# Reordering the hand-over from expert scores to expert outputs, and two operands of the routing copied to PSUM

## The reference, cut to what matters

```python
v1, i1 = lax.top_k(s1, PEER_TOPK)          # 8 heads, 128 keys each, 16 best
v2, i2 = lax.top_k(s2, PEER_TOPK)
cand = (v1[..., :, None] + v2[..., None, :]).reshape(T, PEER_HEADS, 256)
sc, pos = lax.top_k(cand, PEER_TOPK)
eidx = jnp.take_along_axis(cidx, pos, axis=-1)
gate = jax.nn.softmax(sc, axis=-1)
u = jnp.take(u_tab, eb, axis=0)
a = jnp.einsum('nhkd,nd->nhk', u, xb)
w = jax.nn.gelu(a, approximate=False) * gb
vv = jnp.take(v_tab, eb, axis=0)
return jnp.einsum('nhk,nhkd->nd', w, vv)
```

## Time and profile before

| | us |
|---|---|
| median of 3 runs (1568.36 to 1580.45) | 1569.83 |
| the profiled execution | 1577.24 |
| its span, first to last instruction | 1575.6 |
| PE busy in the span | 1510.4 |
| DVE, POOL, ACT busy | 1025.4, 997.6, 652.0 |

### The profile page before, as it was taken

The page is one execution under the profiler, slowest core; times in us unless marked ns, Lnnn a source line. Parts: engine busy times, 40 slices in busy tenths (PEclk is TensorE's granted clock), DMA queues, the critical chain, the costliest instruction groups (busy, mean ns, idle before and its releaser), DMA issues.

```text
span 1575.6 us, 25142 instructions
## 1 busy us (share of the span) xinstructions
PE 1510.4 (96%) x8005; PEld 1348.5 (86%) x8005; DVE 1025.4 (65%) x2027; ACT 652.0 (41%) x1013; POOL 997.6 (63%) x611
## 2 busy tenths in 40 slices
PE   7998989999999989999999999899999999999995
PEld 4777767888999989999999999878888888888884
DVE  5356576588999987776767673465555555555556
ACT  5555562234333344555555554223333333333332
POOL 3313241234686866767676667688888888888873
PEclk9999999999999999999999999999999999999998
DMA  6112130222686878998999899799999999999991
GB/s 221 55 54 94 46 102 1 100 88 85 193 277 207 271 245 311 332 324 320 345 332 327 310 347 346 236 336 343 352 347 345 352 345 341 356 343 344 354 323 54
DMA packets 155442, 397.92 MB, mean 253 GB/s; under 512 B 12992, under 2 KB 77248, under 8 KB 153216
## 3 DMA queue, kind: packets, MB, share of 16 engines
q1 hardware_dynamic: 117936, 262.93, 49.1%
q0 software_dynamic: 37456, 134.37, 22.5%
HBM read 347.12 MB, written 50.14 MB: 252 GB/s over the span
## 4 chain that ended last, share of the span: by engine, by line
PE 78%; DVE 14%; issue 4%; ACT 3%; POOL 1%; DMA 1%; DVEq 0%; ACTq 0%; SPq 0%; POOLq 0%
PE banks L1504 12%; PE banks L1506 12%; PE banks L1505 12%; PE banks L1450 11%; PE banks L1452 11%; PE banks L1451 11%; PE banks L1711 5%; PE banks L1566 2%; DVE cand L1248 1%; DVE sel L1258 1%; DVE work L1253 1%; ACT hi L365 1%; DVE rows L1135 1%; DVE top_i L1223 1%; DVE top_i L1208 1%
## 5 line engine op out<-in xcount | busy, mean ns | idle before, releaser
L371 POOL TENSOR_TENSOR lo<-raw,hi 128x1024 fp32r<-128x1024 f32 x292 | 704.2, 2413 | 447.7 <-ACT hi L365 437.6
L1450 PE MATMUL banks<-x1T_hi,hi 128*128 128x384 f32 (+2 forms) x1168 | 405.0, 347 | 5.4 <-POOL lo L371 5.1
L1452 PE MATMUL banks<-x1T_hi,lo 128*128 128x384 f32 (+2 forms) x1168 | 399.0, 342 | 0.0
L1451 PE MATMUL banks<-x1T_lo,hi 128*128 128x384 f32 (+2 forms) x1168 | 398.7, 341 | 0.0
L365 ACT ACTIVATE hi<-raw 128x1024 fp32r<-128x1024 f32 x292 | 306.0, 1048 | 1.2 <-PE banks L1506 0.7
L1504 PE MATMUL banks<-hi,wgt_hi 128*128 128x512 f32 x768 | 302.3, 394 | 3.6 <-DVE wgt_lo L1359 3.6
L1506 PE MATMUL banks<-hi,wgt_lo 128*128 128x512 f32 x768 | 303.3, 395 | 0.0
L1505 PE MATMUL banks<-lo,wgt_hi 128*128 128x512 f32 x768 | 302.6, 394 | 0.0
L1450 PEld LDWEIGHTS banks<-x1T_hi,hi 128*128 128x128 f32 x1168 | 221.1, 189 | 10.2 <-issue 5.7
L1359 DVE TENSOR_TENSOR wgt_lo<-wgt,wgt_hi 128x384 fp32r<-128x384 f32 x128 | 72.4, 566 | 240.0 <-ACT wgt_hi L901 184.3
L1452 PEld LDWEIGHTS banks<-x1T_hi,lo 128*128 128x128 f32 x1168 | 220.6, 189 | 4.9
(11 more groups left out here) (184 smaller groups left out, 1825.0 us busy)
## 6 DMA issues: line engine op xcount, KB each, us to landing
raw<-u_t SPq DMA_DIRECT2D x128, 512.0 KB
raw<-v_tab SPq DMA_DIRECT2D x128, 512.0 KB
g_scratch<-stage SPq DMA_DIRECT2D x12, 2048.0 KB
gg<-g_scratch SPq DMA_DIRECT2D x32, 768.0 KB
gelu_scratch<-gelu SPq DMA_DIRECT2D x116, 192.0 KB
ga<-gelu_scratch SPq DMA_DIRECT2D x29, 768.0 KB
raw<-w SPq DMA_DIRECT2D x26, 512.0 KB
raw<-w_pq SPq DMA_DIRECT2D x16, 512.0 KB
```

The costliest lines, as they stand in the source:

```text
L371: eng.tensor_tensor(l[:, :], raw[:, c % RAW_SLOTS, :], h[:, :].bitcast(F32), ALU.subtract).then_inc(lo_ready, 1)
L1450: pe.matmul(o, h[:, s], hiT[:, k, tokens], start=(k == 0), stop=False)
L1451: pe.matmul(o, h[:, s], loT[:, k, tokens], start=False, stop=False)
L1452: ins = pe.matmul(o, l[:, s], hiT[:, k, tokens], start=False, stop=(k == KT - 1))
```

## The change

Three parts. In `route_block` an operand of the sum of candidates and one of the gates' logits are copied to PSUM first (`best_1`, `top_1`), with one more wait on `route_step`; ROUTE_STEPS counts them. On DVE the eight dots of round 15 stand ahead of the waits and the first two products, and read `x1_home`; behind wgt_lo of tiles 0 and 1 the products 2 and 3 are made too, and `octet(0)` makes neither again. On ACT the gelu of the dots moves ahead of wgt_hi of tiles 0 and 1, so ahead of the last four gelus of u. PE's wait before v tile 0 asks for all 128 used rows, where it asked for 120, since banks 4 and 5, in which x1_home lies, are written by v tile 0.

```diff
--- before.py
+++ after.py
@@ -81,7 +81,7 @@
 assert len(FIRST_ROWS_AT) == R_PRE * ROWS + AHEAD
 LIST_SLOTS = 4
 LIST_STEPS = 4
-ROUTE_STEPS = 2 + 5 + 2 + 2 + 6
+ROUTE_STEPS = 3 + 5 + 3 + 2 + 6
 X_CHUNKS = 4
 
 
@@ -221,6 +221,8 @@
         iota_home = banks[:, 6, 0:NKEY]
         best_f = banks[:, 6, NKEY:NKEY + LISTS * TOPK].rearrange("p (l k) -> p l k", l=LISTS)
         pos_f = banks[:, 7, 0:2 * P].rearrange("p (s n) -> p s n", s=2)
+        best_1 = banks[:, 7, 2 * P:3 * P].rearrange("p (h k) -> p h k", k=TOPK)
+        top_1 = banks[:, 7, 3 * P:3 * P + PH].rearrange("p (h k) -> p h k", k=1)
         gateT = banks[:, 6, NKEY:NKEY + DENSE]
 
         y0 = banks[:, 0:2, :].rearrange("p h n -> p (h n)")
@@ -902,13 +904,12 @@
 
             for it in range((A_PRE + A_MID) // 4, ETILES // 4):
                 if it == ETILES // 4 - 1:
+                    act.wait_ge(dots8_free, R_ALL + 1)
+                    act.activation(dots_gelu[:, :], dots[:, :], ACT.Gelu).then_inc(dots_gelu_ready, 1)
                     weight_hi(0, 0, True)
                     weight_hi(1, 0, True)
                 for k in range(4):
                     gelu_tile(k, it, keep=4 * it + k - A_PRE - A_MID)
-
-            act.wait_ge(dots8_free, R_ALL + 1)
-            act.activation(dots_gelu[:, :], dots[:, :], ACT.Gelu).then_inc(dots_gelu_ready, 1)
 
             with act.Fori(0, ETILES // 8 - 1) as i:
                 for k in range(8):
@@ -1130,9 +1131,7 @@
                 if k == 0:
 
                     dve.wait_ge(dots8_free, r + 1)
-
-                with_x = x1[:, 0, :] if isinstance(r, int) and r == R_ALL - 1 else x1_home
-                dve.tensor_tensor_reduce(rows[:, k, :], rows[:, k, :], with_x, 1.0, 0.0, ALU.mult, ALU.add,
+                dve.tensor_tensor_reduce(rows[:, k, :], rows[:, k, :], x1_home, 1.0, 0.0, ALU.mult, ALU.add,
                                          dots8[:, k:k + 1]).then_inc(row_used, 1)
 
             def keep_dots(r):
@@ -1229,19 +1228,22 @@
                 step(dve.tensor_copy(best_f[:, :, :], best_i[:, bass.ds(b, 1), :, :].rearrange("p o l k -> p (o l) k")))
 
                 halves = best[:, bass.ds(b, 1), :, :].rearrange("p o (h s) k -> p (o h) s k", s=2)
+                step(dve.tensor_copy(best_1, halves[:, :, 0, :]))
+                begin()
                 step(dve.tensor_tensor(cand[:, :, :].rearrange("p h (i j) -> p h i j", j=TOPK),
-                                       halves[:, :, 0, :].unsqueeze(3).to_broadcast([P, PH, TOPK, TOPK]),
+                                       best_1.unsqueeze(3).to_broadcast([P, PH, TOPK, TOPK]),
                                        halves[:, :, 1, :].unsqueeze(2).to_broadcast([P, PH, TOPK, TOPK]), ALU.add))
                 begin()
                 top16(top, top_i, cand, PH)
                 flat_i = top_i[:, :, :].rearrange("p h k -> p (h k)")
                 step(dve.tensor_scalar(pos_u[:, 0, :], flat_i, 4, None, ALU.logical_shift_right))
                 step(dve.tensor_scalar(pos_u[:, 1, :], flat_i, TOPK - 1, None, ALU.bitwise_and))
+                step(dve.tensor_copy(top_1, top[:, :, 0:1]))
                 begin()
                 step(dve.tensor_copy(pos_f[:, :, :], pos_u[:, :, :]))
 
                 step(dve.tensor_tensor(sel[:, 2, bass.ds(b, 1), :].rearrange("p o (h k) -> p (o h) k", k=TOPK), top[:, :, :],
-                                       top[:, :, 0:1].to_broadcast([P, PH, TOPK]), ALU.subtract))
+                                       top_1.to_broadcast([P, PH, TOPK]), ALU.subtract))
                 begin()
                 ids = best_f[:, :, :].rearrange("p (h s) k -> p h s k", s=2)
                 for s in range(2):
@@ -1360,20 +1362,23 @@
                                   ALU.subtract).then_inc(wgt_lo_ready, 1)
 
             for r in range(R_PRE + R_MID, R_ALL):
-                if r == R_ALL - 1:
-
-                    dve.wait_ge(g_stored[0], 16 * CHUNKS // 2)
-                    dve.wait_ge(g_stored[1], 16 * CHUNKS // 2)
-
-                    dve.wait_ge(gelu_ready, A_PRE + A_MID + 2)
-                    for k in range(2):
-                        weights(k, 0)
-                    for k in range(2):
-                        weight_lo(k, 0)
                 for k in range(ROWS):
                     dot(k, r)
                 keep_dots(r)
 
+            dve.wait_ge(g_stored[0], 16 * CHUNKS // 2)
+            dve.wait_ge(g_stored[1], 16 * CHUNKS // 2)
+
+            dve.wait_ge(gelu_ready, A_PRE + A_MID + 2)
+            for k in range(2):
+                weights(k, 0)
+            for k in range(2):
+                weight_lo(k, 0)
+
+            dve.wait_ge(gelu_ready, A_PRE + A_MID + 4)
+            for k in range(2, 4):
+                weights(k, 0)
+
             dve.wait_ge(dots_gelu_ready, 1)
             dve.tensor_tensor(row_weight[:, :], dots_gelu[:, :], sel[:, 2, 0, :], ALU.mult).then_inc(row_weight_ready, 1)
             dve.wait_ge(row_weight_ready, 1)
@@ -1392,16 +1397,16 @@
             dve.tensor_scalar(y0, x1[:, 0, :], ALPHA, None, ALU.mult).then_inc(residual_ready, 1)
             dve.wait_ge(residual_ready, 1)
 
-            def octet(i, made=0):
+            def octet(i, made=0, split=0):
 
                 for k in range(8):
                     if k >= made:
                         weights(k, i)
                     add_row(k, i)
-                    if k >= made:
+                    if k >= split:
                         weight_lo(k, 2 * i)
 
-            octet(0, made=2)
+            octet(0, made=4, split=2)
             octet(1)
             with dve.Fori(2, OCTETS) as i:
                 octet(i)
@@ -1729,7 +1734,7 @@
 
             pe.wait_ge(staged, DENSE // 4)
 
-            pe.wait_ge(row_used, RANKS - ROWS)
+            pe.wait_ge(row_used, RANKS)
 
             def experts(k, it, start=False, last=False):
```

## The result

The changed kernel takes 1560.82 us (median of 7 runs, 1558.8 to 1562.01). The kernel before, measured again beside it, takes 1572.55 (7 runs, 1568.36 to 1580.45; the 1569.83 shown ahead of the prediction is the median of the first three of them). The medians differ by 11.7 us, 0.7%. The ratio, estimated from all the runs, is 0.9912 with a 95% interval of 0.9893 to 0.993, so 11 to 17 us: 0.9% faster, just within the 1% on either side that the prediction books as no change. The profiled execution took 1561.2 us, with a span of 1559.5 against 1575.6 before, so 16.1 less.

The account below looks back on a forecast made before the run. PE, busy 1510.4 of 1575.6 us, was taken as the bound, so only its stalls and low clock could pay. Gains 7.5+6.1+4.7 = 18.3 us, 17.3 taken from the median 1569.83, gave 1552.5, range 1545 to 1565.

Parts of the forecast that it names:

- The stall of POOL, 7.5 us: Before u tile 125: moving round 15's dots ahead ends POOL's 11.50 us stand and PE's late start, gaining 7.5 us.
- The slower rival: Last u tiles: gelus wait behind a late gathered row, each us after 1002 costing PE one plus clock; chance 0.04.
- The start of v, 6.1 us: Before the third v tile: PE's 3.6 us wait for wgt_lo and its clock loss mostly go, gaining 6.1 us.
- Products 2 and 3 are made near 1001 to 1003: At the hand-over to v: DVE makes these products early, in time in which it has nothing else.
- The rival in which v stays late: Start of v: wgt_lo of products 0 to 2 runs into POOL's lo and PE stops, 1560.6 us; chance 0.16.
- The routing, 4.7 us: End of routing: two copies to PSUM save DVE 3.9 us net, bringing PE 4.7 with the clock, from 1.2 to 5.2.
- 3.9 less brings PE 3.9: End of routing: DVE is late by 4.16 us, so its 3.9 us saving reaches PE in full.
- PE's wait for L1299 is under 1 us: End of routing: sign that the forecast is right; the wait was 4.16 us before.
- The 0.8 added for the clock: After PE's wait at the routing's end: lower clock costs 0.3 us seen at one product plus an estimated 0.5.
- The rival that the prediction set beside the rule of the Trainium skill: Routing: stalls move to integer lines L1238 and L1239, so it gives nothing, 1556.2 us; chance 0.17.
- I take 17.3 from the median: 1552.5: Whole kernel: of the 18.3 us sum, 17.3 is taken off the three-run median of 1569.83.
- DMA sets the pace: v stage: the earlier start only makes v wait for loads, leaving the routing's gain, 1565.1 us; chance 0.06.

Follow-up runs that it names:

- dots_only: Kernel before with only round 15's dots moved (x1_home, their gelu, PE's wait), no copies, two products ahead: 1562.54 us, ratio 0.993.
- two_products: Changed kernel with only products 0 and 1 made ahead instead of four: 1558.8 us, ratio 0.9896 to the kernel before.
- no_copies_look2: The changed kernel without the two copies to PSUM, profiled a second time: 1563.91 us.
- pos_psum: Changed kernel with the integer results pos_u in PSUM as well: 1559.87 us, ratio 0.9897 to the kernel before.
- no_copies: Changed kernel without the two copies to PSUM: 1560.82 us, ratio 0.9916 to the kernel before.
- two_early: Changed kernel with two products ahead, pos_u in PSUM and ACT's exponential of the gates before the gelu of tile 41: 1558.21 us, ratio 0.9884 to the kernel before.
- copies_only: Kernel before with the two copies to PSUM and nothing else: 1572.88 us against 1575.86, ratio 0.9983.
- before_look1: Kernel before, unedited, profiled in a second execution: 1576.73 us.
- four_products: Kernel before with products 2 and 3 also made ahead, round 15's dots still behind them: 1573.99 us against 1575.21, ratio 1.000.

## Why the prediction was right, and where it was not

**The stall of POOL, 7.5 us: right.** Measured 7.6. The gathers were done as read from the earlier trace rows. Shifted by the 2.7 us by which this stage now comes earlier (1.27 later, 4.0 won), the forecast last landing at 996 is 993.3, and the dot ran at 992.81. The products ended at 995.28 against a shifted 995.9. The slower rival needed rows later than 1002, shifted 999.3; the last came six us sooner. dots_only shows the cause: it differs from the kernel before in nothing but the dots' place and what goes with it (x1_home, their gelu, PE's wait), and ACT's idle before tile 125 is 1.67 where it was 10.19.

**The start of v, 6.1 us: right in size (5.8), wrong in its cause.** The prediction gave it to "Products 2 and 3 are made near 1001 to 1003". two_products and dots_only, without them, have 12.4 us where the changed kernel has 13.1. So the stall went with the dots' place and what goes with it. The timelines point to one part of that, the gelu of the dots. In the kernel before it came at 1022.02, behind the last u gelu, and y0 only at 1023.12, 2.7 us after that gelu; now y0 starts 0.6 after it (1010.74 and 1010.14). With 2.1 us in hand product 2 also misses the lo that had held it for 3.41 us, but narrowly: in two_products POOL's lo ends at 1012.33 and the product starts at 1012.85. POOL's own timing differs as well, since its stand of 11.50 us is gone, and no run moves the gelu or POOL's timing alone; how the gain divides between them is not shown. Making products early tends to a loss of 0.7: in three of the four traces with four products and the dots ahead (the changed kernel, no_copies_look2, pos_psum) three sums in a row put the third wgt_lo onto POOL's lo, 13.1 us; in the fourth, no_copies, it missed the lo, 12.4. The three with two products (two_products, dots_only, two_early) all have 12.4. The prediction saw exactly that collision ("0 to 1 us of stall remains"), but not that the plain order has none. The rival in which v stays late did not come.

**The routing, 4.7 us: 4.0, and partly by chance.** DVE gained 4.0 where 3.9 were forecast, and that agreement is in part luck. The two changed lines gave back 5.6 as forecast (5.7); the copies, at 0.28 and 0.16 us, and the wait on the own semaphore, 0.5 in all, cost 2.2 instead of 1.8. That leaves 3.4; 1.0 came from shorter stalls of the integer lines, which the sum did not have, and 0.4 was lost elsewhere. The term that was too large is the wait: "3.9 less brings PE 3.9" gave 3.0, since ACT's exponential took over as the bound, which the prediction had not looked for; pos_psum shows it, with 6.7 us less on DVE and nothing on PE. So "PE's wait for L1299 is under 1 us" fell, at 1.16, with 0.42 for ACT's copy behind it. The 0.8 added for the clock was about right: 1.0 came behind the wait. The rival that the prediction set beside the rule of the Trainium skill (SBUF — State Buffer, Who interferes with whom) was that the integer lines, which have both sides in SBUF, would take the stall over. They did keep theirs, 6.1 and 3.1 us for four each, but these are together 1.0 less than before. The runs agree with the rule itself: with their results in PSUM (pos_psum) the same lines take 0.29 and never more. What the rule does not tell is how often two engines meet. Of six traces without the copies five have a route of 167.6 and one has 163.5; the three with the copies and pos_u in SBUF (the changed kernel, copies_only, two_products) have 163.5 to 163.6. The short one is not short for want of the stall that the copies remove: the sum of candidates took 4.38 or 4.39 us in block 1 in all six. It is short at the integer lines. Why both ways end at the same 163.5 was not tried. If such executions are common, the copies are worth less than 4.0 on average; the 3.0 of copies_only (0.8 to 4.7) fits that, and fits 4.0 too.

**The sum and its base: here most of the miss arose.** By the trace 18.3 were forecast and 17.35 came. The forecast's own first figure, the profiled 1577.24 less 18.3, was 1558.9 against 1561.2 now: 0.95 from the sum, 1.27 from the attention stages. The measured 1560.82 is 8.3 above the forecast. The step that failed is "I take 17.3 from the median: 1552.5". The median of three runs was a poor base: with more runs the same kernel gave 1572.55 (7, those three among them), 1575.86 (17), 1575.21 (17) and 1571.88 (9). The alternative stood in the text, and was to be preferred: before_look1 shows the stalls at the same size in a second execution, 1576.73 us long. The medians' difference of 11.7 is itself under the trace's 16.1, though 16.1 lies within the 11 to 16.8 of the ratio's interval. Part of it may be the routing's chance above, and part is the base again, since two_products, 0.7 us from the changed kernel by the trace, stands 17.1 under its 1575.86. The rest was not settled. Some of it sits in how the attention stages vary from run to run: the routing starts between 395.20 (no_copies) and 401.49 (pos_psum) in these traces. PE's largest wait there (for `probs`) comes to 9.2 to 11.4 us in all, its others differ by 1 us or less. The granted clock differs too. From 100 to 200 us and from 200 to 300 it is 1.00 and 0.98 in no_copies, 0.95 and 0.98 in the kernel before (start at 399.56), 0.95 and 0.95 in the changed kernel (400.83). Why it fell in one execution and not in another stays open.

**DMA sets the pace: fell.** No engine waits for a transfer in the v stage, and 1050 to 1100 has the same rate as before. Just ahead of it the earlier order is nearer to that limit: ACT waits 1.17 us for a tile of v at 999.33 in the changed kernel, and 2.96 at 995.50 in no_copies, both hidden from PE (its longest wait for a lo is 0.5 and 0.6).

**Chances.** The forecast put 0.58 on faster by over 1% and 0.39 on within 1%, where the result is. Its own gain was 1.1%, the trace's 16.1 us are 1.02% and the ratio says 0.9%: nothing here could tell the sides of that line apart, and 0.58 leaned on a sum set against too low a base. The range of 1545 to 1565 holds the time.

## What to carry to other kernels

When an engine waits long for one thing, look at what is queued behind the wait and gets its data sooner: moving eight dots, whose rows arrive in the course of a 27 us wait, ahead of it was worth 13 of the 17 us, and the two products made early beside it, which help only where the dots stay last, cost 0.7 in most traces. Ask which other engine's instruction must move too; here y0 could not start before the gelu of the dots on ACT, which had stood behind the last gelu of u. When a stall seems to be gone, look whether it is the one that the edit was aimed at: the route was 4.1 us shorter once without the copies, at other lines. And apply a sum read from one profiled execution to that execution's own time, above all where the few runs at hand scatter by as much as the gain.

## What was not expected of the hardware

A dot (`tensor_tensor_reduce`) is held by POOL like any other instruction with two SBUF operands. Durations in ns of all 128 in the changed kernel, x1 in PSUM, and of the eight with x1 in SBUF in four_products:

```profile
L1134 DVE CUSTOM_DVE_ANT_0 rows<-rows,banks x128: 1198/1216/1222, 481.5 to 992.8; 128x1024 f32<-128x1024 f32 x128
```

```profile
L1135 DVE CUSTOM_DVE_ANT_0 rows<-rows,x x8: 1214/1218/3402, 999.7 to 1009.9; 128x1024 f32<-128x1024 f32 x8
```

In PSUM none of 128 was held; in SBUF two of eight took 3.35 and 3.40 us. So reading x1_home in the last round, as the change does, removes a stall of its own kind as well. What that is worth was not measured apart: no run has the dots ahead with x1 in SBUF.

Where POOL had waited 0.75 us more in block 1, DVE ended the routing 4.1 us sooner. The same program without the copies took 163.50 and 167.59 us for the same route, and in the six traces without the copies nothing between was seen. Whether the 0.75 us alone made the difference was not tried.
